# Projections multiplied in fp32 straight from an eight-slot weight ring, modulation weights streamed under the S5 scan

## What is computed

```python
mod = jax.nn.silu(c) @ w_ada[l] + b_ada[l]                 # 2048 x 12288
shift1, scale1, gate1, shift2, scale2, gate2 = jnp.split(mod[:, None, :], N_MOD, axis=-1)
h = rms_norm(x, norm1_gain[l]) * (1 + scale1) + shift1
x = x + gate1 * mixing_sublayer(h, w_in[l], ...)           # three attentions, gated, then @ w_out
h = rms_norm(x, norm2_gain[l]) * (1 + scale2) + shift2
x = x + gate2 * swiglu(h, w_ffn_in[l], w_ffn_out[l])
```

## Time and profile before

| | |
|---|---|
| median of 3 runs | 4340.76 us (4335.61 to 4342.26) |
| the profiled execution's own time | 4344.78 us |
| its span | 4343.0 us |
| TensorE busy | 2622.9 us (60%), 10288 records |
| VectorE / ScalarE / GpSimd busy | 2543.3 / 797.9 / 1548.3 us |
| HBM read | 1016.59 MB |

### The profile page before, as it was taken

How to read it: one execution, slowest core, us unless ns; L and a number is a source line. 1 busy time by engine, 2 the same in 40 slices (tenths; PEclk the granted TensorE clock), 3 DMA queues, 4 the chain that set the end, 5 groups by cost and what they waited for, 6 DMA issues and landing times. The chain is left out here.

```text
span 4343.0 us, 29024 instructions
## 1 busy us (share of the span) xinstructions
PE 2622.9 (60%) x10288; PEld 1814.1 (42%) x10288; DVE 2543.3 (59%) x2726; ACT 797.9 (18%) x670; POOL 1548.3 (36%) x669
## 2 busy tenths in 40 slices
PE   6899489354200000000001999989899879999999
PEld 4455367100000000000001888433677667888787
DVE  1887644977788888888886443635010154444444
ACT  1000233000000000000001333211333324433333
POOL 0000000078888888888883000000677500000000
PEclk9899699677555555555555999899999989999999
DMA  5233044299999999999995555467444444555554
GB/s 157 78 116 107 34 165 157 78 365 414 415 386 390 393 378 378 381 379 378 383 389 210 194 193 174 145 216 253 159 168 166 158 171 166 192 186 191 175 193 164
DMA packets 331962, 1020.04 MB, mean 235 GB/s; under 512 B 37192, under 2 KB 37800, under 8 KB 264416
## 3 DMA queue, kind: packets, MB, share of 16 engines
q1 hardware_dynamic: 258128, 481.90, 32.6%
q0 software_dynamic: 73728, 536.90, 31.0%
q10 hardware_dynamic: 16, 0.02, 0.0%
HBM read 1016.59 MB, written 2.16 MB: 235 GB/s over the span
## 5 line engine op out<-in xcount | busy, mean ns | idle before, releaser
L314 DVE TENSOR_TENSOR slab_low<-ring,slab_high 128x2048 fp32r<-128x2048 f32 x240 | 549.6, 2292 | 715.2 <-ACT slab_high L308 715.2
L294 PE MATMUL bank<-slab_high,left_high 128*128 128x512 f32 x1952 | 771.5, 395 | 69.4 <-POOL slab_low L314 34.4
L515 PE MATMUL bank<-ident,nat 128*128 128x128 f32 x128 | 22.9, 363 | 1295.0 <-DVE nat L496 1257.3
L308 ACT CAST slab_high<-ring 128x2048 fp32r<-128x2048 f32 x304 | 579.6, 1909 | 1090.2 <-PE bank L296 1019.9
L295 PE MATMUL bank<-slab_low,left_high 128*128 128x512 f32 x1952 | 764.9, 392 | 0.0
L296 PE MATMUL bank<-slab_high,left_low 128*128 128x512 f32 x1952 | 764.3, 392 | 0.0
L1403 DVE CUSTOM_DVE_ANT_0 pool<-pool,nat 128x2048 f32<-128x2048 f32 x256 | 586.6, 2295 | 145.5 <-DMA pool<-in_peer_u,small 137.8
L1414 DVE SCALAR_TENSOR_TENSOR res<-pool,res 128x2048 f32<-128x2048 f32 x256 | 603.3, 2356 | 99.5 <-DMA pool<-in_peer_v,small 71.8
L1436 POOL DMA_INDIRECT pool<-in_peer_u,small x256 | 602.4, 2353 | 96.7 <-issue 68.3
L1436 POOL DMA_INDIRECT pool<-in_peer_v,small x256 | 551.2, 2153 | 96.7 <-issue 68.3
L515 PEld LDWEIGHTS bank<-ident,nat 128*128 128x128 f32 x128 | 22.0, 196 | 1296.9 <-DVE nat L496 1258.8
(11 more groups left out here) (458 smaller groups left out, 2601.8 us busy)
## 6 DMA issues: line engine op xcount, KB each, us to landing
ring<-in_w_in SPq DMA_DIRECT2D x148, 1024.0 KB, 4.9
ring<-in_w_ada SPq DMA_DIRECT2D x96, 1024.0 KB, 5.0
ring<-in_w_ffn_in SPq DMA_DIRECT2D x88, 1024.0 KB, 4.8
ring<-in_w_ffn_out SPq DMA_DIRECT2D x44, 1024.0 KB, 5.0
ring<-in_w_out SPq DMA_DIRECT2D x32, 1024.0 KB, 5.0
ring<-in_peer_wq SPq DMA_DIRECT2D x16, 1024.0 KB, 5.1
ring<-in_w_br_gla SPq DMA_DIRECT2D x8, 1024.0 KB, 4.9
pool<-modulation SPq DMA_DIRECT2D x5, 1024.0 KB, 6.8
```

Of the source, the lines that this page charges most:

```text
L294: nc.tensor.matmul(o, lh, high[:, part, k, :], start=first, stop=False)
L308: nc.scalar.copy(high[:, n % PARTS], ring[:, g % SLOTS]).then_inc(high_done, 1)
L314: eng.tensor_tensor(low[:, n % PARTS], ring[:, g % SLOTS], high[:, n % PARTS].bitcast(F32), ALU.subtract)\
L515: last = nc.tensor.transpose(ps[n][:, j * P:(j + 1) * P], dst[:, t, k * P:(k + 1) * P], ident[:, :])
```

## The change

It has three parts. (1) `high`, `low` and everything that fills them are gone; every projection multiplies the fp32 slab in the ring by an fp32 left operand, 8 matmuls a slab (`slab`, new L248). (2) The ring has 8 slots, in the place of 4 and two buffer pairs, so eight slabs are loaded ahead of a section. (3) The 96 modulation slabs (24 rows of 512 outputs, 4 slabs a row) leave the attention blocks: 16 rows are multiplied in the S5 chunks, two a chunk, and 8 in the routing block. Each of a slab's four matmuls now has 32 columns of weights (31 of them zero) and writes its own strip of 32 partitions of one bank; VectorE adds the bank up in `mod_acc` and four products with the identity add the strips at the end. Smaller: the copies of the left operand are shared between ScalarE and VectorE, the narrow product of `MIX` is made once and not in two halves, and `c` is loaded at the start of the kernel.

```diff
-SLOTS = 4
-PARTS = 2
+SLOTS = 8
...
+        w_ada = a["w_ada_2"][0]
+        ROWS = NMOD * OB
+        PER_CHUNK = 2
+        ROWS_S5 = PER_CHUNK * (4 * W // NB)
+        ROWS_ROUTE = ROWS - ROWS_S5
...
-            Section(4 * W // NB, 4, plain(w_in)),
+            Section((1 + PER_CHUNK) * (4 * W // NB), 4, qkvo_and_ada),
...
-        def slab(pe, g, outs, lhs, k0, start, stop):
-
-            pe.wait_ge(low_done, split_index(g) + 1)
-            last = slab_products(split_index(g) % PARTS, outs, lhs, k0, start, stop)
-            last.then_inc(slabs_used, 1)
...
+        def slab(pe, g, outs, lhs, k0, start, stop, i=None):
 
             slot = g % SLOTS
+            pe.wait_ge(landed[slot], reach[g] if i is None else i * 16 + reach[g])
             for k in range(KS):
                 for o, t in outs:
+                    last = nc.tensor.matmul(o, lhs(k0 + k, t), ring[:, slot, k, :], start=start and k == 0,
+                                            stop=stop and k == KS - 1)
             last.then_inc(slabs_used, 1)
...
-            nc.scalar.copy(high[:, n % PARTS], ring[:, g % SLOTS]).then_inc(high_done, 1)
...
-            eng.tensor_tensor(low[:, n % PARTS], ring[:, g % SLOTS], high[:, n % PARTS].bitcast(F32), ALU.subtract)\
-               .then_inc(low_done, 1)
...
+        def modulate(pe, g, row, bank, first=True, final=True):
+
+
+            for m in range(4):
+                slot = (g + m) % SLOTS
+                pe.wait_ge(landed[slot], reach[g + m])
+                for k in range(KS):
+                    last = nc.tensor.matmul(ps[bank][32 * k:32 * k + 32, :], spread[:, 4 * m + k, 31 - row:63 - row],
+                                            ring[:, slot, k, :], start=first and m == 0, stop=final and m == 3)
+                last.then_inc(slabs_used, 1)
...
+                sp.dma_start(stat[:, 0:KD], a["c_2"][0].rearrange("(k p) -> p k", p=P), allow_slow_non_contiguous=True)\
+                  .then_inc(s_cl, 16)
                 for m in range(SLOTS):
                     issue(sp, U_, m, m)
                 sp.wait_ge(s_x, 16)
...
                     pe.wait_ge(s_rot, c + 1)
+                    for r in range(PER_CHUNK):
+                        modulate(pe, g0 + step * c + 4 * (r + 1), PER_CHUNK * c + r, 3, r == 0, r == PER_CHUNK - 1)
                     pe.wait_ge(s_blkc, c + 1)
...
+                dve.wait_ge(slabs_used, first_slab[ADA_R + 1])
+                v.tensor_tensor(mod_acc, mod_acc, ps[0][:, :], ALU.add).then_inc(s_mtk, 1)
                 for q in range(4):
...
-                whole_linear(pe, ADA_A, s_mtk, lambda k: ccol[:, k:k + 1])
+                for r in range(ROWS_ROUTE):
+                    modulate(pe, g0 + 4 * r, ROWS_S5 + r, 0, r == 0, r == ROWS_ROUTE - 1)
+                pe.wait_ge(s_mtk, 1)
+                for k in range(KS):
+                    last = nc.tensor.matmul(ps[1][0:32, :], ident[:, 32 * k:32 * k + 32], mod_acc,
+                                            start=k == 0, stop=k == KS - 1)
+                last.then_inc(s_msum, 1)
...
-                        for h in range(2):
-                            last = nc.tensor.matmul(ps[4][:, t * GR:(t + 1) * GR], left(k, t)[h].bitcast(F32),
-                                                    wa[:, k, :], start=k + h == 0, stop=k + h == KD)
+                            last = nc.tensor.matmul(ps[4][:, t * GR:(t + 1) * GR], left(k, t), wa[:, k, :],
+                                                    start=k == 0, stop=k == KD - 1)
...
-        BESIDE = {"heads": (3, 1), "stick": (5, 3, 0), "dilated": (5, 2, 0), "gla": (5, 5, 3, 4, 3, 4, 3, 4, 3, 5, 6)}
...
-                modulate(pe, BESIDE["gla"][0])
                 pe.wait_ge(s_gs, gm["aT"])
```

More of the change, by code:

```diff
@@ L208, in build @@
             first_slab.append(first_slab[-1] + s.n)
[L210 to L226, removed]
         def issue(sp, sec, n, g):
             s = SECTIONS[sec]
-            slot_free(sp, g)
+            if g >= SLOTS:
+                sp.wait_ge(slabs_used, g - SLOTS + 1)
             for k0, ks, src in s.source(n // s.per, n % s.per):
@@ L287, in whole_slab @@
             last.then_inc(slabs_used, 1)
-        def slab_products(part, outs, lhs, k0, start, stop, ks=range(KS)):
-            for k in ks:
-                for o, t in outs:
-                    lh, ll = lhs(k0 + k, t)
-                    first, final = start and k == 0, stop and k == KS - 1
-                    nc.tensor.matmul(o, lh, high[:, part, k, :], start=first, stop=False)
-                    nc.tensor.matmul(o, lh, low[:, part, k, :], start=False, stop=False)
-                    last = nc.tensor.matmul(o, ll, high[:, part, k, :], start=False, stop=final)
-            return last
@@ L317, in high_blocks @@
[L317 to L333 removed]
+        def left(k, t):
+            return aT[:, k, t * P:(t + 1) * P]
@@ L347, in pair @@
                     for j in range(KD // KS):
-                        m = p * (KD // KS) + j
-                        pe.wait_ge(low_done, i * 8 + (n0 + m + 1))
-                        last = slab_products((n0 + m) % PARTS, [(ps[p * TT + t][:, :], t) for t in range(TT)], lhs,
-                                             j * KS, j == 0, j == KD // KS - 1)
-                        last.then_inc(slabs_used, 1)
+                        slab(pe, g0 + p * (KD // KS) + j, [(ps[p * TT + t][:, :], t) for t in range(TT)], lhs,
+                             j * KS, j == 0, j == KD // KS - 1, None if first else i)
             pair(0, True)
@@ L585, in _ @@
                     for j in range(4):
-                        whole_slab(pe, g0 + 4 * b + j, [(ps[2 * b + t][:, :], t) for t in range(TT)], 4 * j,
-                                   j == 0, j == 3)
+                        slab(pe, g0 + 4 * b + j, [(ps[2 * b + t][:, :], t) for t in range(TT)], left, 4 * j,
+                             j == 0, j == 3)
                 pe.wait_ge(s_wg, 16)
@@ L1178, in _ @@
                     linear(pe, sec, [taken])
-                @block.scalar
-                def _(act):
-                    high_blocks(act, sec, lambda b: None)
                 @block.vector
                 def _(dve):
-                    def add(b):
+                    for b in range(s.blocks):
                         dve.wait_ge(slabs_used, g0 + 4 * (b + 1))
@@ L2210, in _ @@
                     last.then_inc(s_gd, 1)
-                for x in range(done, SECTIONS[GATES].n):
-                    high_part(act, g0 + x)
             @block.vector
```

510 lines of the change are left out of this document (144 added, 366 removed).

## The result

The changed kernel takes **4648.5 us** (median of 4 runs, 4644.8 to 4664.1) against 4340.4 us before (4 runs as well): 1.072 times as long, 95% interval 1.069 to 1.075. The profiled execution has a span of 4649.7 us, 306.7 more than the one before.

What follows compares the result with a forecast made beforehand. The prediction took TensorE to bound the projections, with the split hidden. 342 + 45 - 53 + 110 - 29 - 30 + 12 + 7 = +404 us on a span of 4343, forecast 4745 us; range 4690 to 4865.

Steps and rivals of the forecast that it cites:

- Modulation in the S5 chunks: In the S5 chunks: 32 added matmuls lengthen each chunk, 1.72 us a slab, 13.7 us a chunk, +110 us.
- all four strips at once: Rival, chance 0.25: in the S5 chunks records of other strips don't wait; +55 us, 4690 to 4710 us.
- The bounds (+55 and +220): Modulation in the S5 chunks: +55 us with four strips at once, +220 us with matmuls one behind the other.
- 1.3 us a slab: S5 chunks: slab cost estimated from the skill page's 2.38x, making the modulation term some 80 us.
- Attention blocks: Attention blocks: 70 us won where TensorE came back late, about 44 lost to cooling; sum -29 us (-10 to -60).
- Direct products: Projections outside `GATES`: 240 slabs go from 5.44 to 6.87 us each, +342 us.
- `GATES`: `GATES` projection: 64 slabs go from 402.7 us to 448 us, +45 us.
- Gathers: Expert gathers: 78 gathers no longer run beside slabs and take 215 us, not 248; -30 us.
- narrow product: `MIX`: the narrow products lasted 23.8 us and half of them remain, -14 us.
- kernel start: Kernel start: four more slabs and `c` lie ahead of the first gain row, +12 us.
- stage starts: Projection starts: the first slab no longer waits for its two parts, 4.3 us at six stages.
- VectorE's new wait ahead of the dots: Routing block: forecast free; rival, chance 0.03: at the low clock 32 slabs take 220 us, delaying dots 105 us.

Runs made afterwards that it cites:

- Experiment 2: Changed kernel with the four matmuls of each modulation slab alternating between two strips (0 and 1 in even slabs, 2 and 3 in odd); 4655.0 us, 1.071 times before.
- experiment 1: Changed kernel with the modulation's strip chosen by the slab, so a slab's four matmuls write one strip; 4714.2 us, 1.085 times before.
- experiment 5: Changed kernel with eight unused filler matmuls on TensorE behind each full GLA level; 4642.1 us, 1.067 times before.
- Experiment 7: Kernel before, split products kept and nothing moved, with attention-block modulation written to four strips that VectorE adds; 4299.7 us, 0.989 times before.
- experiment 6: Changed kernel with TensorE's start in `W_OUT2` held back by twelve ScalarE copies; 4661.7 us, 1.074 times before.
- experiment 8: Kernel before with modulation in four strips in both attention blocks and routing block, split products kept; 4256.9 us, 0.980 times before.
- Experiment 4: Changed kernel with four of eight slabs issued behind the first gain row and behind the convolution's weights; 4631.9 us, 1.065 times before.

## Why the prediction was wrong

- **Modulation in the S5 chunks: this step failed.** The prediction said "records leave in order, so only the second of one strip and the first of the next run together", and took 0.43 us a matmul. The trace has 0.22 us a matmul (7.07 us for 32), the case "all four strips at once" with its +55: it measured +55.1. Experiment 2 contradicts the order, and experiment 1 shows that it is the strips that overlap and that the look ahead is short. The bounds (+55 and +220) held; the choice between them was an argument and no row, and the likeliest sum rested on it. The Trainium skill (TensorE: Matmul & The Clock Gate, Part 3) says that matmuls start and end strictly in program order. The trace disagrees for these fp32 matmuls: with two strips in turn that order would give 10.3 us at the least, and 7.25 were measured. The Trainium skill's 2.38x for three column strips of 512 columns (same page, Measured speedup vs the span model) says rightly that strips overlap; here it was 3.43 / 0.88 = 3.9x for four. The prediction's 1.3 us a slab does not follow from that 2.38x: 3.43 / 2.38 is 1.44 us, 92 us for 64 slabs and not 80 (an estimate from that page).
- **Attention blocks: right mechanism, half the size.** Of the -60.1 us, 9.1 are the start of `GATES` (10.15 us of idle, now 1.03), so the blocks themselves gave 51. If TensorE's lateness was worth the 73 us that were read, cooling cost some 22 and not 44. What is measured: the 458 records of the blocks' own products were busy 62.6 us before and 90.6 us now, 28 more in all and not 62.6, since only a part of them ran at the low clock; and 14 of the 22 are the levels (experiment 5). The term was too high because it doubled every product that nothing else paced. Experiment 7 won 46 us with no slab moved: what paid was for the most part the shorter modulation, not its absence. (Of the 96 modulation slabs only 64 stood in the attention blocks before the change; 32 were in the routing block already.)
- **Direct products: right, 13 us too high.** 0.43 us a record and 16 records a slab held everywhere (`MIX` 412.1 us for 60 slabs). The old 5.44 us a slab had been cleared of its slow first products, but they were not put back as something that the change removes. The changed stages begin after 1 us of idle at the full clock, and experiment 6 gives 2.3 us a stage for that, times six, 14 us.
- **Gathers: right, 10 us too low.** Three of the ten are the sum's own: 248 less 215 is 33, and it took 30. The 2.76 us of the earlier trace rows divided a window by its instructions; the last 177 dot products of the kernel before start 2.73 us apart (1139.5 to 1619.5 us), all 256 of the changed one 2.72 and those of experiment 8 2.69. Two executions of one program differ by up to 10 us in the gathers (experiment 7 reaches `MIX` 10.7 us later than the kernel before, with the same instructions until then), so the rest is at the edge of what can be told.
- **`GATES`, narrow product, kernel start:** +45.9, -15.1 and +11.2 us against +45, -14 and +12 less copies. The six other stage starts gave 34 us and not 26: their idle time went from 6.1 to 7.7 us each to 1.03 to 1.05, where the prediction took 4.3 us a stage from one chain. That is the small gap in the last row but one of the table.
- **Missed: the convolution's weights,** +12.3 us. The prediction counted what lies ahead of the norms' rows on the queue, and not what lies ahead of the one small load between the S5 chunks and mLSTM. Experiment 4 shows the cause: with four slabs of the eight issued behind them the wait is 4.56 us and not 15.22.
- VectorE's new wait ahead of the dots never bit (33.8 us to spare), and no stage of the changed kernel waited for slabs but the routing block, where 2.71 us a slab is the transfers' pace.

The sum of the errors, -55, -25, -13, -10 and +12, and some 6 us of small gaps, is the 97 us that the forecast was too high. The first alone takes the time from 4745 to 4690, the lower end of the range. It leaves the range by the terms behind it, which all but one went the same way; so the rival with all four strips at once, 4690 to 4710 us, had the right strips and missed as well.

## What to carry to other kernels

Count records, not matmuls: an fp32 product costs two records where three fp32r products cost three of half the length, so dropping a hidden split made a projection that TensorE bounds a quarter longer (`MIX` 412.1 us, 328.7 before). A one-row product is cheap if its matmuls go to different strips of 32 partitions of a bank: four row chunks then take the time of one, and it pays at once wherever such products stand in somebody's wait. When a ring gets deeper, look at each small load that is issued behind it.

## What was not expected of the hardware

- Fp32 matmuls on four strips start four at a time, 0.03 us or less apart, every 0.43 us; alternating between two strips costs nothing (7.25 us for 64 records), eight records in a row on one strip cost 15.85 us, so TensorE starts records of another strip ahead of queued ones of a busy strip, though only a few ahead.
- In the levels TensorE's own 16 products took 2.05 us where fillers of 7.03 us and gaps of 1.9 us lay ahead of them (experiment 5), and 3.78 us behind strips of 3.6 us and gaps of 5 us (experiment 7): strips that take a third of the time also let the engine fall to the lower clock. The granted clock over the levels was 1.00 in the kernel before (2893.79 to 3010.04 us) and 0.77 in experiment 7 (2889 to 2967 us).
